# Attention in 64-query pieces, and the second gated branch added by VectorE, in an fp32 hybrid encoder step on one core

## The chip, the cores and the metric

One NeuronCore of a Trainium2 chip runs the whole program. The metric is device time in microseconds of one execution. The kernel before takes 1704.32 us (median of three runs, 1704.09 to 1705.3).

## What is computed

One step of an encoder layer for 1024 prompt tokens and 64 sample tokens (1088 in all), with D = 1024, in float32. The parts that matter here:

```python
proj = rmsnorm(x) @ w_in                      # u, v_g, q, k, v, gates
# attention: 16 query heads, 4 key heads, head dim 64, 64-query chunks,
# each sees its own chunk of keys and the two chunks (128 keys) before it
s = q @ k.T * 64**-0.5 - slope[head] * abs(distance)
m = max(max(s), sink[head]);  e = exp(s - m)
p = e / (sum(e) + exp(sink[head] - m));  o = p @ v
# sample tokens: one 64-query chunk over 128 cached keys and its own 64
merged = sigmoid(g_A) * (A @ w_pa) + sigmoid(g_B) * (B @ w_pb)   # A gated MLP, B = o
x = x + merged @ w_o
x = x + (gelu(conv3(h2 @ w_up_gate)) * (h2 @ w_up_val)) @ w_down
y = rmsnorm(x)
```

## The kernel before

**Products.** All large products have the weight as TensorE's stationary operand and the transposed activations as the moving one. Both are split into a high and a low fp32r part, and three of the four part products are made (hi hi, hi lo, lo hi). The work is cut into 56 "pairs" of 128 output channels each (`NPAIR`, L39): pairs 0 to 21 are the input projection, 22 to 25 `w_pb` ("pb"), 26 to 29 `w_pa` ("pa"), 30 to 33 `w_o` ("out"), 34 to 55 `w_up` ("up"). A pair treats its weight and activation as 2x2 blocks. A plain pair (0, 1, 22, 26 to 34) makes eight block products, the others seven by the Strassen-Winograd form, from sums of blocks that VectorE makes. The four results are called quadrants Q11, Q21, Q12, Q22; in PSUM there are three regions for them. One block product is 24 matmuls of 128x272 in four groups of six (`product`, L2123). After the pairs comes the down projection: 20 rounds of four tiles, one round per 512x256 block (L2330), and a last part in other order (L2367).

**The order** is written out by hand. Every engine walks the same grid (pair p, slot n of seven, quarter j of four), and hangs its own work on fixed places: `base`, `background` and `operands` of each engine. A tick is one quarter. TensorE puts side work between the groups of six matmuls in `background` (L2273).

**Attention** is such side work: 36 steps i, (key head b = i // 9, query tile n = i % 9), one every ten ticks (`ATT_STEP`, L134) from tick 96 on. A step takes 128 queries of the four heads of one key head. For prompt tiles 1 to 7 the keys are two tiles of 128, for n = 0 one, and for n = 8 (the sample) 128 cached and 64 own; a key outside a query's window is masked by a huge entry in the distance table, which GpSimd writes (`windows`, L1028). A head e is 2h + k; h = 0 sits on partitions 0 to 63 of the q and k tiles and h = 1 on 64 to 127.

- SyncE: `load_qk` (L777) one load of q and two of k, `load_v` (L799) one load of v per key tile, `store_o` (L812).
- TensorE: `scores` (L2193) four matmuls with 64 contraction rows, q stationary, 256 keys moving; `transpose_p` (L2208) one transpose per head and key tile, eight in a full step; `attend` (L2219) v stationary (64 columns), the transposed shares moving, for h and then for the key tile; h = 1 writes the lower 64 PSUM partitions:

```python
for h in range(2):
    for j, rows in enumerate(tiles):
        last = pe.matmul(side[64 * h:64 * h + 64, 0, 0:256].rearrange("p (k q) -> p k q", k=2),
                         v_now[0:rows, s, j, :], pt_sb[0:rows, j, 2 * h:2 * h + 2, :],
                         start=j == 0, stop=j == len(tiles) - 1)
```

- VectorE: `maxima` (L1709), `shares` (L1730). ScalarE: `exponents` (L1239), `p_out` (L1247, two 128x512 copies), `o_out` (L1255).

An f32 matmul stands in the trace as two records of its full width (x8 for four matmuls), a transpose as one.

**Operands of a stage.** When a stage begins, ScalarE makes the high parts of the seven operand blocks (`operand_hi`, L1145) and VectorE the sums (`t_sum`, L1557) and low parts (`operand_lo`, L1542, L1555). The places are tables in `operands` of each engine (L1377, L1854). For pb the low parts of blocks 5 and 4 are made within pair 22, the plain one, which doesn't use them.

**Gating.** In the pa stage VectorE multiplies each quadrant with its sigmoid gate (`gate_a`, L1790), and GpSimd adds the stored B quadrant (`merge`, L1046, add at L1052) at slots 3, 6 and, for two of the four, at the start of the next pair. The merged quadrants are the operands of the out stage: ScalarE's `operand_hi` waits for their count. The quadrant buffers are freed by it for the loads of the gates, of the B quadrants (L696 on) and of the residual (`load_residual`, L719). At the end of a pair of the out stage VectorE adds the residual to a quadrant (`residual_out`, L1666, L1674), which also frees the PSUM region for the next pair's first product.

**Down projection.** ScalarE, in order after the last pair: `convolve(21)`, `gelu(21)` (L1358, waits for both filter taps of VectorE), `down_hi_part(1)` (L1362), and so on. VectorE: the add of tile 0 to `xy` (L2015), second tap (L1830), `down_lo_part(1)` (L1844), the add of tile 1. TensorE has two PSUM sets, so tile t waits for the add of tile t - 2.

## Time and profile before

| what | value |
|---|---|
| median of the runs | 1704.32 us |
| the profiled execution | 1703.68 us, its span 1701.6 us |
| mean granted TensorE clock in it | 0.994 |
| busy share of the span | TensorE 98%, weight loads 95%, VectorE 66%, ScalarE 40%, GpSimd 5% |
| attention steps | from 118 us to 517 us |
| pb, pa, out, up stages | from 656, 745, 841 and 940 us |
| down projection | from 1412.7 us |

Times are microseconds from the start of the span. The time of the execution holds about 2 us around the span. PE is TensorE's matmuls, PEld its weight loads (which can run beside them), DVE VectorE, ACT ScalarE, POOL GpSimd, SP SyncE; a q behind a name is that engine's queue of DMA issues. "Idle before" is time in which the engine did nothing ahead of an instruction, with what released it.

### The profile page before, as it was taken

The numbers are of one execution on the slowest core, as the hardware profiler recorded it, in microseconds if no ns is written. First come the engines' busy times: TensorE is split into PE (matmuls) and PEld (weight loads), VectorE is DVE, ScalarE is ACT, GpSimd is POOL, SyncE is SP. The second block draws the span as 40 slices with busy tenths as digits, with TensorE's granted clock in tenths as the row PEclk, the third lists the DMA queues.
The fourth block names the chain that finished last, engine by engine and source line by source line (L and its number), as shares of the span: only waits on it lengthen the run. The fifth ranks groups of instructions, "written<-read, shape, count | busy, mean of one in ns | idle before, by whom it ended". The sixth has DMA issues, their size and how long they took to land.

```text
span 1701.6 us, 31439 instructions
## 1 busy us (share of the span) xinstructions
PE 1665.7 (98%) x12566; PEld 1610.8 (95%) x12566; DVE 1116.4 (66%) x2044; ACT 674.3 (40%) x1240; POOL 84.3 (5%) x143
## 2 busy tenths in 40 slices
PE   6999999999999999999999999999999999999997
PEld 6998888888889999999999999999999999999996
DVE  6666566565656878652434887777777776666665
ACT  7344454454444336442434543333333333111112
POOL 2000000000000000002212300000000000000001
PEclk8999999999999999999999999999999999999999
DMA  8443434234345855575344222222222235222122
GB/s 249 138 152 115 123 97 136 86 119 119 107 119 156 257 176 200 181 240 156 90 149 136 64 76 77 77 77 77 77 76 77 77 116 209 103 90 102 66 75 106
DMA packets 240579, 209.40 MB, mean 123 GB/s; under 512 B 24759, under 2 KB 197619, under 8 KB 240435
## 3 DMA queue, kind: packets, MB, share of 16 engines
q1 hardware_dynamic: 125806, 149.64, 26.5%
q10 hardware_dynamic: 114629, 57.76, 12.1%
q8 instruction: 100, 1.64, 0.4%
q14 instruction: 44, 0.36, 0.1%
HBM read 141.91 MB, written 65.45 MB: 122 GB/s over the span
## 4 chain that ended last, share of the span: by engine, by line
PE 75%; DVE 3%; issue 2%; ACT 1%; DMA 1%; DVEq 0%; POOL 0%; SPq 0%; ACTq 0%
PE ps L2130 55%; PE ps L2330 14%; PE ps L2225 1%; PE ps L2367 1%; PE ps L2204 1%; PE ps L2250 1%; PE ps L2216 1%; DMA r<-o_spill 1%; DVE op_lo L1555 1%; PE ps L2240 0%; PE ps L2349 0%; ACT sc_sb L1243 0%; DVE sc_sb L1721 0%; DVE y_sb L2035 0%; DVE w_lo L1516 0%
## 5 line engine op out<-in xcount | busy, mean ns | idle before, releaser
L2130 PE MATMUL ps<-op_hi,w_hi 128*128 128x272 f32 x3232 | 683.9, 293 | 11.4 <-issue 4.8
L2130 PE MATMUL ps<-op_hi,w_lo 128*128 128x272 f32 x3232 | 669.7, 289 | 0.0
L2130 PE MATMUL ps<-op_lo,w_hi 128*128 128x272 f32 x3232 | 667.8, 288 | 0.0
L2130 PEld LDWEIGHTS ps<-op_hi,w_hi 128*128 128x128 f32 x3232 | 507.4, 189 | 38.7 <-issue 36.6
L2130 PEld LDWEIGHTS ps<-op_lo,w_hi 128*128 128x128 f32 x3232 | 508.7, 189 | 0.0
L2130 PEld LDWEIGHTS ps<-op_hi,w_lo 128*128 128x128 f32 x3232 | 506.1, 189 | 0.0
L1516 DVE TENSOR_TENSOR w_lo<-raw,w_hi 128x512 fp32r<-128x512 f32 x224 | 153.5, 703 | 190.7 <-ACT w_hi L1143 190.7
L1143 ACT ACTIVATE w_hi<-raw 128x512 fp32r<-128x512 f32 x224 | 134.6, 625 | 124.5 <-PE ps L2130 90.2
L2015 DVE TENSOR_TENSOR xy<-ps,xy 128x728 f32<-128x728 f32 (+1 forms) x160 | 108.4, 719 | 79.3 <-PE ps L2330 79.3
L1220 ACT ACTIVATE u<-ps 128x544 f32<-128x544 f32 x88 | 54.8, 623 | 178.6 <-PE ps L2130 178.6
L1243 ACT ACTIVATE sc_sb<-sc_sb,att_stat 128x256 f32<-128x256 f32 (+2 forms) x144 | 69.0, 480 | 109.8 <-DVE att_stat L1727 109.8
L2330 PE MATMUL ps<-g_hi,d_hi 128*128 128x364 f32 (+1 forms) x480 | 106.7, 331 | 2.7 <-DVE xy L2015 2.6
L2330 PE MATMUL ps<-g_lo,d_hi 128*128 128x364 f32 (+1 forms) x480 | 106.3, 330 | 0.0
L2330 PE MATMUL ps<-g_hi,d_lo 128*128 128x364 f32 (+1 forms) x480 | 106.3, 330 | 0.0
L1366 ACT ACTIVATE d_hi<-d_raw 128x1024 fp32r<-128x1024 f32 x22 | 23.3, 1060 | 195.1 <-PE ps L2330 185.4
L1516 DVE TENSOR_TENSOR w_lo<-w_f,w_hi 128x512 fp32r<-128x512 f32 x132 | 87.0, 685 | 4.0 <-ACT w_hi L1143 3.4
L1143 ACT ACTIVATE w_hi<-w_f 128x512 fp32r<-128x512 f32 x132 | 78.9, 625 | 25.6 <-DVE w_f L1536 21.8
L2330 PEld LDWEIGHTS ps<-g_hi,d_hi 128*128 128x128 f32 x480 | 83.6, 189 | 3.5 <-DVE xy L2015 3.3
L2330 PEld LDWEIGHTS ps<-g_hi,d_lo 128*128 128x128 f32 x480 | 83.7, 189 | 0.0
L2330 PEld LDWEIGHTS ps<-g_lo,d_hi 128*128 128x128 f32 x480 | 83.7, 189 | 0.0
L1654 DVE TENSOR_TENSOR quad<-u,ps 128x544 f32<-128x544 f32 x69 | 49.4, 716 | 29.5 <-ACT u L1220 18.4
L1721 DVE CUSTOM_DVE_ANT_0 sc_sb<-ps,bias,sinks 128x256 f32<-128x256 f32 (+2 forms) x144 | 57.9, 459 | 0.3 <-issue 0.3
(176 smaller groups left out, 1587.5 us busy)
## 6 DMA issues: line engine op xcount, KB each, us to landing
in_spill<-quad SPq DMA_DIRECT2D x88, 272.0 KB, 2.1
raw<-in_w_up_dram ACTq DMA_DIRECT2D x44, 512.0 KB, 4.8
raw<-in_w_in_dram ACTq DMA_DIRECT2D x42, 512.0 KB, 5.7
g_spill<-value_out SPq DMA_DIRECT2D x22, 544.0 KB, 2.7
g_in<-g_spill SPq DMA_DIRECT2D x11, 1088.0 KB, 5.8
d_raw<-in_w_down_dram SPq DMA_DIRECT2D x22, 512.0 KB, 3.4
q_now<-in_spill SPq DMA_DIRECT2D x36, 128.0 KB, 2.4
gate_q<-in_spill SPq DMA_DIRECT2D x16, 272.0 KB, 8.2
```

The costliest lines, as they stand in the source:

```text
L1143: act.activation(w_hi[n][:], weight_source(p, n), copy).then_inc(s_w_hi, 1)
L1220: act.activation(two((m1c, u2, u3)[i][:]), reg[0][:, :, 0:HB], copy).then_inc(s_copied, 1)
L1243: act.activation(sc_sb[:, i % 2, e, 0:w], sc_sb[:, i % 2, e, 0:w], ACT.Exp, bias=a[:, 1, e:e + 1], accum_out=a[:, 3, e:e + 1])
L1366: act.activation(d_hi[:, blk % 2, :], d_raw[:, blk % 2, :], copy).then_inc(s_d_hi, 1)
L1516: dve.tensor_tensor(w_lo[n][:], weight_source(p, n), w_hi[n][:].bitcast(F32), ALU.subtract).then_inc(s_w, 1)
L1555: dve.tensor_tensor(op_lo[at][:, j], operand_source(g, n)[:, j], op_hi[at][:, j].bitcast(F32), ALU.subtract).then_inc(s_op, 1)
L1654: dve.tensor_tensor(two(out), two(first[:]), reg[region][:, :, 0:HB], op).then_inc(s_comb, 1)
L1721: last = dve.tensor_tensor_reduce(sc_sb[:, i % 2, e, 0:w], side[:, e // 2, 256 * (e % 2):256 * (e % 2) + w], bias[:, e, b0:b0 + w], HD ** ...
L2015: last = dve.tensor_tensor(d, v, d, ALU.add)
L2130: last = pe.matmul(out[:, h, 0:HB], (w_hi, w_lo)[a][place][:, j, :], (op_hi, op_lo)[b][at][:, j, HB * h:HB * h + HB], start=fresh and j == ...
L2204: last = pe.matmul(side[:, h, 256 * k:256 * k + w], q_now[64 * h:64 * h + 64, s, k, :], k_now[64 * h:64 * h + 64, s, 0:w], start=True, sto ...
L2330: last = pe.matmul(pset[t % 2][:, blkn, 0:t1 - t0], (d_hi, d_lo)[x][:, blk % 2, 512 * k + P * q:512 * k + P * q + P], (g_hi, g_lo)[y][g % ...
```

## The change

Four things are changed.

1. **Attention by 64 queries of two heads.** The 128 stationary columns of a score matmul are now 64 queries of both heads k = 0 and 1; a step of a full tile has two query chunks c and two h. Each chunk sees exactly its 192 keys (`SPAN`), so nothing is masked, and for n = 0 the keys that don't exist are left out (`seen`). For n = 8 there is one chunk only. The table of distances is made without GpSimd's window masks and with an added VectorE operation. The scores are 192 keys wide. Each head pair's shares are transposed in a 128-key and a 64-key part ("own"); the own parts of chunk 0 and 1 are copied to partitions 0 to 63 and 64 to 127 of a tile, and `attend` becomes four matmuls of 128 rows and four of 64 rows, all 128 columns wide, alternating in h. The copies become one of 128x512 and two of 64x256. SyncE issues two loads of q for one, and three of v for two.
2. **Merge by VectorE**, at slots (3,2), (6,1), (6,3) and (0,2) of the next pair.
3. **Low parts moved.** For pb, the low parts of blocks 5 and 4 go from pair 22 to pair 23, (0,2) and (1,2). For out and up, that of block 7a goes from (5,1) to (6,1) of the last pair ahead of the stage.
4. **ScalarE's `down_hi_part(1)`** comes before `gelu(FT - 1)`.

```diff
+def chunks_of(n):
+
+    return (0, 1) if n < NT - 1 else (0,)
+
+
+def seen(n, c):
+
+    return WINDOW - CHUNK * c if n == 0 else 0
...
-                sp.dma_start(q_now[:, s], in_spill[2 * Q_PAIR + 2 * b:2 * Q_PAIR + 2 * b + 2, :, q0:q0 + P]
-                             .rearrange("k p t -> p k t")).then_inc(s_qk_in[s], 16)
+                for c in chunks_of(n):
+                    q0 = n * P + CHUNK * c
+                    sp.dma_start(q_now[:, s, c, :].rearrange("p (k q) -> p k q", k=2),
+                                 in_spill[2 * Q_PAIR + 2 * b:2 * Q_PAIR + 2 * b + 2, :, q0:q0 + CHUNK].rearrange("k p t -> p k t"))\
+                      .then_inc(s_qk_in[s], 16)
...
-                    for m in range(len(key_rows(n))):
-                        k0 = keys_of(n)[0] + m * P
+                    for m in range(3) if n else (2,):
+                        k0 = (n - 1) * P + CHUNK * (0, 1, 2)[m]
                         sp.dma_start(v_now[:, s, m, :], vt_spill[k0:k0 + P, cols]).then_inc(s_v_in[s], 16)
...
-                if PA <= p < OUT and j == 0 and n in (3, 6):
-                    merge(4 * (p - PA) + {3: 0, 6: 1}[n])
-                if PA < p <= OUT and j == 0 and n == 0:
-                    merge(4 * (p - 1 - PA) + 2)
-                    merge(4 * (p - 1 - PA) + 3)
...
-                for j, rows in enumerate(key_rows(i % NT)):
-                    last = act.activation(pt_sb[0:rows, j, :, :], side[0:rows, j, :].rearrange("p (e q) -> p e q", e=4), copy)
+                n = i % NT
+                turned_p, own = side[:, 0, :].rearrange("p (h c q) -> p c h q", h=2, c=2), side[0:CHUNK, 1, :].rearrange("p (c q) -> p c q", c=2)
+                pt = pt_sb[:].rearrange("p (h c) q -> p c h q", h=2)
+                if 0 < n < NT - 1:
+                    act.activation(pt_sb[:].rearrange("p e q -> p (e q)"), side[:, 0, :], copy)
+                else:
+                    act.activation(pt[:, n == 0], turned_p[:, n == 0], copy)
+                for c in chunks_of(n) if n else (0,):
+                    last = act.activation(pt_own[CHUNK * c:CHUNK * c + CHUNK].rearrange("p h q -> p (h q)"), own[:, c], copy)
...
             convolve(FT - 1)
+            down_hi_part(1)
             gelu(FT - 1)
             for g in range(FT // 2):
-                down_hi_part(2 * g + 1)
+                if g:
+                    down_hi_part(2 * g + 1)
                 if g + 1 < FT // 2:
...
-                for e in range(4):
-                    head = 4 * b + 2 * (e % 2) + e // 2
-                    last = dve.tensor_tensor_reduce(
-                        sc_sb[:, i % 2, e, 0:w], side[:, e // 2, 256 * (e % 2):256 * (e % 2) + w], bias[:, e, b0:b0 + w],
-                        HD ** -0.5, sinks[:, head:head + 1], ALU.add, ALU.max, a[:, 0, e:e + 1])
+                for h in range(2):
+                    for c in chunks_of(n):
+                        e, w0 = 2 * h + c, seen(n, c)
+                        last = dve.tensor_tensor_reduce(
+                            sc_sb[:, i % 2, e, w0:SPAN], side[:, h, SPAN * c + w0:SPAN * c + SPAN], bias[:, h, w0:SPAN],
+                            HD ** -0.5, sinks[:, b, h:h + 1], ALU.add, ALU.max, a[:, 0, e:e + 1])
...
+            def merge(i):
+
+                p, q = i // 4, numbered(PA, i)[1]
+                dve.wait_ge(s_gated, i + 1)
+                dve.wait_ge(s_mb_in[i % 3], 16 * (i // 3 + 1))
+                dst = r_q[q][:, p, :]
+                dve.tensor_tensor(dst, dst, mb_buf[i % 3][:], ALU.add).then_inc(s_merged, 1)
...
-                            lows = {(1, 3): ((0, "a"),), (2, 1): ((3, "a"),), (2, 3): ((1, "a"),), (3, 3): ((0, "b"),), (5, 1): ((7, "a"),),
+                            lows = {(1, 3): ((0, "a"),), (2, 1): ((3, "a"),), (2, 3): ((1, "a"),), (3, 3): ((0, "b"),), (6, 1): ((7, "a"),),
...
-                            lows = {(1, 2): ((6, "w"),), (2, 0): ((3, "w"),), (3, 0): ((2, "w"),), (4, 2): ((5, "w"),), (5, 2): ((4, "w"),)}
+                            lows = {(1, 2): ((6, "w"),), (2, 0): ((3, "w"),), (3, 0): ((2, "w"),)}
...
-                    if (p, g) == (2, 0):
+                    if g < 3 and p == lead(g) + 1 and summed(g):
                         lows = {(0, 2): ((5, "w"),), (1, 2): ((4, "w"),)}
...
+                if stage(p) == "pa" and (n, j) in ((3, 2), (6, 1), (6, 3)):
+                    merge(4 * (p - PA) + {(3, 2): 0, (6, 1): 1, (6, 3): 2}[n, j])
+                if PA < p <= OUT and (n, j) == (0, 2):
+                    merge(4 * (p - 1 - PA) + 3)
...
-                for k in range(2):
+                for c in chunks_of(n):
                     for h in range(2):
-                        last = pe.matmul(side[:, h, 256 * k:256 * k + w], q_now[64 * h:64 * h + 64, s, k, :],
-                                         k_now[64 * h:64 * h + 64, s, 0:w], start=True, stop=True)
+                        w0 = seen(n, c)
+                        last = pe.matmul(side[:, h, SPAN * c + w0:SPAN * c + SPAN], q_now[64 * h:64 * h + 64, s, c, :],
+                                         k_now[64 * h:64 * h + 64, s, CHUNK * c + w0:CHUNK * c + SPAN], start=True, stop=True)
                 last.then_inc(s_sc, 1)
...
+                n = i % NT
+                for h in range(2):
+                    for c in chunks_of(n):
+                        e, x = 2 * h + c, sc_sb[:, i % 2, 2 * h + c]
+                        if n or c:
+                            pe.transpose(side[:, 0, e * P:e * P + P], x[:, 0:WINDOW] if n else x[:, CHUNK:SPAN], ident[:])
+                for h in range(2):
+                    for c in chunks_of(n) if n else (0,):
+                        last = pe.transpose(side[0:CHUNK, 1, (2 * c + h) * P:(2 * c + h) * P + P], sc_sb[:, i % 2, 2 * h + c, WINDOW:SPAN],
+                                            ident[:])
...
-                for h in range(2):
-                    for j, rows in enumerate(tiles):
-                        last = pe.matmul(side[64 * h:64 * h + 64, 0, 0:256].rearrange("p (k q) -> p k q", k=2),
-                                         v_now[0:rows, s, j, :], pt_sb[0:rows, j, 2 * h:2 * h + 2, :],
-                                         start=j == 0, stop=j == len(tiles) - 1)
+                for c in chunks_of(n):
+                    for h in range(2):
+                        if n or c:
+                            last = pe.matmul(side[64 * h:64 * h + 64, c, 0:P], v_now[:, s, c if n else 2, :], pt_sb[:, 2 * h + c, :],
+                                             start=True, stop=n == 0)
+                for c in chunks_of(n) if n else (0,):
+                    for h in range(2):
+                        own = slice(CHUNK * c, CHUNK * c + CHUNK)
+                        last = pe.matmul(side[64 * h:64 * h + 64, c, 0:P], v_now[own, s, 2, :], pt_own[own, h, :], start=n == 0, stop=True)
```

## Rows read from the trace of the kernel before

**Rows 1.** Busy by stretch: us, PE, PEld, DVE, ACT, POOL, PEclk, DMA share, GB/s

```profile
200.00:300.00 100.00, 99.76 (x764) 88.34 (x763) 60.78 (x205) 49.13 (x141) 0.00 (x0) 1.00 0.40 117
```

**Rows 2.** Who waited for whom on PE (total us, times, longest)

```profile
PE ps L2225 <- ACT pt_sb L1252: 2.2, 3, 0.8
```

**Rows 3.** Timeline of PE: the matmuls at four joints that waited

```profile
681.78 0.49 PE L2130 MATMUL ps<-op_hi,w_hi 128*128 128x272 f32 x2 [1.59 <-ACT quad L1309]
...
854.50 0.49 PE L2130 MATMUL ps<-op_hi,w_hi 128*128 128x272 f32 x2 [0.86 <-DVE quad L1674]
...
940.24 0.49 PE L2130 MATMUL ps<-op_hi,w_hi 128*128 128x272 f32 x2 [1.31 <-DVE quad_x L1674]
...
1424.92 1.27 PE L2330 MATMUL ps<-g_hi,d_hi 128*128 128x364 f32 x3 [2.62 <-DVE xy L2015]
```

**Rows 4.** Chain of waits, steps 34 and 35 (start us, us, what)

```profile
487.34 1.06 PE ps L2204 x8
...
491.62 0.87 PE ps L2216 x8
...
494.75 1.02 PE ps L2225 x8
...
498.23 0.85 PE ps L2204 x8
...
511.91 0.87 PE ps L2216 x8
...
515.03 2.30 PE ps L2225 x8
```

**Rows 5.** Timeline of PE around side work of steps with n = 0

```profile
213.26 0.71 PE L2204 MATMUL ps<-k_now,q_now 64*128 64x128 f32 x8
213.91 0.52 PE L2130 MATMUL ps<-op_hi,w_hi 128*128 128x272 f32 x2
...
331.08 0.65 PE L2225 MATMUL ps<-pt_sb,v_now 128*64 128x256 f32 x4
331.67 0.52 PE L2130 MATMUL ps<-op_hi,w_hi 128*128 128x272 f32 x2
```

**Rows 6.** Timeline of weight loads in the attend of step 35

```profile
515.54 0.19 PEld L2225 LDWEIGHTS ps<-pt_sb,v_now 64*64 64x64 f32 x2 [0.38 <-issue]
```

**Rows 7.** Who waited for whom on SP, 120 to 500 us

```profile
SPq L667 <- DVE quad L1654: 200.4, 49, 9.3
```

**Rows 8.** Timeline of DVE and ACT before 681.78

```profile
676.76 2.42 DVE L1555 TENSOR_TENSOR op_lo<-lo_f,op_hi 128x2176 fp32r<-128x2176 f32 x1
...
680.30 2.42 DVE L1555 TENSOR_TENSOR op_lo<-r,op_hi 128x2176 fp32r<-128x2176 f32 x1
...
681.03 0.61 ACT L1309 ACTIVATE quad<-ps 128x544 f32<-128x544 f32 x1
```

**Rows 9.** Timeline before 854.50: POOL, DVE, ACT, SP

```profile
842.71 1.74 POOL L1052 TENSOR_TENSOR r<-r,quad 128x544 f32<-128x544 f32 x1 [7.55 <-DVE r L1797]
843.14 1.88 DVE L1797 TENSOR_TENSOR r<-r,m1c 128x544 f32<-128x544 f32 x1
844.54 0.66 ACT L1175 ACTIVATE op_hi<-r 128x544 fp32r<-128x544 f32 x1 [4.01 <-POOL r L1052]
...
848.32 3.89 SPq L732 DMA_DIRECT2D quad<-xt_spill  x4
```

**Rows 10.** Timeline of DVE before 940.24

```profile
937.61 1.85 DVE L1555 TENSOR_TENSOR op_lo<-r,op_hi 128x1632 fp32r<-128x1632 f32 x1
939.38 0.71 DVE L1674 TENSOR_TENSOR quad_x<-quad_x,ps 128x544 f32<-128x544 f32 x1
```

**Rows 11.** Before 1424.92: ACT, DVE; the stretch after, columns of rows 1

```profile
1420.28 1.12 ACT L1360 ACTIVATE conv<-conv 128x1090 f32<-128x1090 f32 x1 [3.95 <-DVE conv L1830]
...
1422.37 1.22 DVE L1846 TENSOR_TENSOR d_lo<-d_raw,d_hi 128x1024 fp32r<-128x1024 f32 x1 [2.13 <-ACT d_hi L1366]
...
1424.90:1428.00 3.10, 3.08 (x10) 3.08 (x11) 3.10 (x4) 0.00 (x0) 0.00 (x0) 0.51 0.00 0
```

More of the change, by code:

```diff
@@ L17 @@
 CACHE = 128
+CHUNK, WINDOW = 64, 128
+SPAN = WINDOW + CHUNK
 HEADS, KVH, HD = 16, 4, 64
@@ L246, in qk_loads @@
 def qk_loads(i):
-    return sum(5 if m % NT == NT - 1 else 3 for m in range(i % 2, i + 1, 2))
+    return sum(5 if m % NT == NT - 1 else 4 for m in range(i % 2, i + 1, 2))
 def v_loads(i):
-    return sum(len(key_rows(m % NT)) for m in range(i % 2, i + 1, 2))
+    return sum(1 if m % NT == 0 else 2 if m % NT == NT - 1 else 3 for m in range(i % 2, i + 1, 2))
 def program(nc, x_prompt, x_sample, cache_k, cache_v, cache_conv, ln_mix_g, w_in, ln_v_g, ln_v_b, w_s, b_s,
@@ L757, in values_back @@
                 sp.dma_start(kc_in[:], cache_k[0, 0].rearrange("t h d -> t (h d)")).then_inc(s_k_in, 16)
-                sp.dma_start(sinks[:], attn_sinks.broadcast_to([P, HEADS])).then_inc(s_sinks, 16)
+                for k in range(2):
+                    sp.dma_start(sinks[CHUNK * k:CHUNK * k + CHUNK],
+                                 attn_sinks.rearrange("a (b k h) -> a k b h", b=KVH, k=2)[:, k].broadcast_to([CHUNK, KVH, 2]))\
+                      .then_inc(s_sinks, 16)
             def values_out():
@@ L1736, in shares @@
                 dve.wait_ge(s_den, 2 * i + 2)
-                for e in range(4):
-                    p = sc_sb[:, i % 2, e, 0:w]
-                    last = dve.tensor_scalar(p, p, a[:, 6, e:e + 1], None, ALU.mult)
+                for h in range(2):
+                    for c in chunks_of(i % NT):
+                        e, x = 2 * h + c, sc_sb[:, i % 2, 2 * h + c, seen(i % NT, c):SPAN]
+                        last = dve.tensor_scalar(x, x, a[:, 6, e:e + 1], None, ALU.mult)
                 last.then_inc(s_p, 1)
```

101 lines of the change are left out of this document (40 added, 61 removed).

## The prediction

> **What bounds the kernel now.** I read the busy time by stretch first: in a typical 100 us of the attention part TensorE is busy 99.76 us, VectorE 60.78 and ScalarE 49.13 [rows 1]. So a TensorE instruction saved there is time saved, and the other engines matter only where TensorE waits for them. Next, who made it wait: in the attention steps 2.2 us, for ScalarE's copies of the transposed shares [rows 2]; and four stops at stage joints, of 1.59, 0.86, 1.31 and 2.62 us [rows 3]. Then the chain of waits through two steps, which is TensorE from end to end: scores 1.06 us, transposes 0.87, attend 1.02 in a full step, and 0.85, 0.87 and 2.30 in the step of the sample tile, n = 8 [rows 4]. The reader should see that the sample tile's attend costs over twice that of a full tile, with the same eight records.
>
> **How a side group is priced.** Score groups of eight records take 1.06 us at 256 columns and 0.85 at 192 [rows 4], and 0.65 at 128 (213.26 to 213.91) [rows 5]. The difference is 0.21 us per 64 columns. Eight records at one column each per cycle of 2.4 GHz would give that sum, and so would four at half that rate, with the two h beside each other. Attend tells the two apart. In a full step, where both h are at hand, four matmuls of 256 columns take 1.02 us [rows 4]. At n = 8 the order is 128 rows, 64 rows, 128 rows, 64 rows, and they take 2.30, or 0.575 each [rows 4]; before each change of shape the weight load stands still for 0.38 us [rows 6]. So an array half handles a record in N x 0.833 ns, halves run side by side, and a run of one shape costs a fixed piece: group = r x N x 0.833 ns + c, with r records per half. Scores: c = 0.21 (4 x 0.213 + 0.21 = 1.06). Attend: c = 0.17 from 1.02 with r = 4; 0.16 from the 0.59 of n = 0 with r = 2 (331.08 to 331.67) [rows 5]; 0.15 from 0.575. I take 0.15 per run of one shape.
>
> The Trainium skill, TensorEngine Tiling (Array Packing), Key Properties, says that a change of tiling mode drains the engine, while tiles of one mode work independently. It speaks against the change: every attend gets a change of mode that full steps didn't have. By that rule, the trace agrees, with its 0.38 us stops; the price is in c already.
>
> **Attention, TensorE.** There are 28 full steps, four with n = 0, four with n = 8.
> - Scores, full: now exactly the form of the old n = 8 group, 0.85 for 1.06: -0.21 x 28 = -5.9. For n = 8 two matmuls of 192: 2 x 0.16 + 0.21 = 0.53 for 0.85, x 4 = -1.3. For n = 0 the widths 64 and 128 for two of 128: between 0 and -0.12 each; the weight load of 128 columns may bind, so -0.05 x 4 = -0.2.
> - Transposes: eight before and after in a full step, and half of the old n = 8 ones were of 64 keys too and the group took the same 0.87 [rows 4]: 0. For n = 8 four fewer at 0.87 / 8 = 0.109: -0.44 x 4 = -1.75. For n = 0 none.
> - Attend, full: four matmuls of 128 rows, r = 4 at 128 columns: 0.43 + 0.15 = 0.58. Then four of 64 rows, one in each quarter of the array if row halves run side by side as they do in the scores: r = 2, 0.21 + 0.15 = 0.36. Together 0.94 for 1.02: -0.08 x 28 = -2.2. If the row halves take turns, r = 4: 1.16, +0.14 x 28 = +3.9. No row shows quarters; I take the first, since halves run beside each other in both directions. For n = 8: 0.36 + 0.36 = 0.72 for 2.30, x 4 = -6.3. For n = 0: 0.72 for 0.59, x 4 = +0.5.
>
> Sum -17.1; with the other value -11.0.
>
> **Attention, other engines.** Scores, exponents and shares get a quarter narrower and two of four fall away at n = 8. The three copies in place of two, and a faster TensorE, can make attend wait more for ScalarE. The 2.2 us of waits [rows 2] may vanish or double; I take 0. SyncE issues two more loads per step, past the stores of quadrants; its queue stands 200.4 us in this part waiting for VectorE's quadrants [rows 7], so there is room, and the loads are issued twelve ticks, over a step, ahead. Nothing for these, nor for the distance table, which comes long before its use. Without that cover each late load would stop TensorE before its group.
>
> **The four joints.**
> - 681.78, start of pair 23. TensorE waits for ScalarE's quadrant copy (681.03 to 681.64), and ScalarE had waited for VectorE's weight sums, behind the two low parts of 2.42 us at 676.76 and 680.30 [rows 8]. The first of these stands ahead of the sum and goes to pair 23, where blocks 4 and 5 are first used in the fifth and sixth product, over 12 us in. VectorE gets free 2.4 us earlier for a stop of 1.59: -1.6. Next late would be those low parts: 4.8 us in 12.
> - 854.50, in pair 30. TensorE waits for a residual add, and that for its load, issued at 848.32 [rows 9] when the last gating freed the buffer. ScalarE stood 4.01 us for the merge on GpSimd (842.71, 1.74 us); beside it a gating on VectorE took 1.88 us [rows 9] where a like operation takes 0.71 [rows 10]. With the merge on VectorE right behind its gating, at 0.71, the high part goes out some 2 us earlier, but VectorE now has the 1.85 us of block 7a and two merges in that place. I walk VectorE's queue: the last gating comes near 847.4 in place of 847.6 to 848.3, the load 0.8 us earlier: -0.8. Sixteen merges add 16 x 0.71 = 11 us to VectorE over 100 us in which it has room; they sit behind loads of the B quadrants made a slot or more before.
> - 940.24, start of pair 34. TensorE waits for the residual add at 939.38, which stands behind block 7a's 1.85 us [rows 10]. Moved behind it: -1.3. The sums and low parts of the up stage follow in pair 34 on VectorE, so between none and all of this may come back as a later stop. I keep -1.3.
> - 1424.92. VectorE stood 2.13 us for the high part of the second block, as ScalarE made it after the gelu of 1420.28, which waits for VectorE's second tap [rows 11]. With the order turned those 2.13 go; the next adds are then some 0.4 late: -1.7 of 2.62. After the stop the granted clock was 0.51 for 3.1 us (1.2 GHz in place of 2.4) [rows 11], which lost 3.1 x 0.49 = 1.5 us. After stops of 1.59 us and less there was no such stretch at the joints, so I take -1.5 as well. Bounds for the joint: -1.1 to -4.1.
>
> Sum of the joints: -1.6 - 0.8 - 1.3 - 3.2 = -6.9.
>
> **Total.** -17.1 - 6.9 = -24.0 against 1703.68 for the profiled execution (span 1701.6): 1679.7. The median is 0.6 above it, so 1680.3; I say 1680.
>
> **Rivals.**
> 1. *Row halves take turns* in the new 64-row matmuls: +6.1, 1686. For: no row has four small blocks at once. Against: score groups of both row halves cost no more per column than a single one.
> 2. *The joints don't pay*: the stops come back behind VectorE, whose work is moved and not less, or attend waits longer for three copies. Half the joints' gain lost and the waits doubled: +3.5 + 2.2, 1686. For: at three of the joints the stop ends on VectorE's work or a wait behind it.
> 3. *Slower: no halves side by side in attend.* With h alternating from one matmul to the next, each of the eight would follow the last: r = 8 at 128 columns, 0.86 + 0.15 = 1.0 per shape and 2.0 for 1.02 in 28 steps, +27.4; n = 8: 0.58 x 2 for 2.30, -4.6; n = 0: 1.16 for 0.59, +2.3. In all +25.1 for the -8.0 above: 1713. It decides in attend, from about 0.85 us over today's 1.02 on. For: the old n = 8 group ran one by one. Against: there the shape changed each time; the old full group had the h one after the other in program order and still ran them side by side. The Trainium skill's page TensorE: Matmul & The Clock Gate, Part 3, has it that matmuls start and end in strict program order. [...]
> 4. *It doesn't do what it says*, for example TensorE's saving is given back as waits for loads or for VectorE: within 0.2% of before, 1702 to 1707.
>
> **Chances.** Forecast 0.63, its own range 1675 to 1684 (waits -2.2 to +2.2, joints -1 to +2). Rival 1 0.13, rival 2 0.13, both together (1692) 0.03, rival 3 0.04, other slower ways 0.02, rival 4 0.02. A range of 1674 to 1691 leaves about 2 in 10 out with my own doubt of the prices. About 0.2% is what a measurement of this kernel can tell from no change: faster 0.92, same 0.02, slower 0.06.
>
> **What would show it.** Right: full attend near 0.94 us (x16), full scores 0.85, sample attend near 0.7; no stop over 0.5 us at the first three joints, one under 1.3 in the down projection and no stretch there at half clock. Attend at 1.16 is rival 1, at 2.0 rival 3. Wrong: stops of TensorE ahead of scores or attend that add up to over 5 us, or pairs 34 to 36 with new stops.

## The result and the profile after

The changed kernel took 1687.97 us, beside 1704.34 for the kernel before: ratio 0.9893, 95% interval 0.9871 to 0.9915. That median counts one slow execution of 4100.05 us, which no experiment here explains and which the ratio leaves out; the four others took 1681.86 to 1688.63, median 1687.31. Run again (after_again) it took 1687.08, from 1683.04 to 1690.88, beside 1703.74: 0.9898 (0.9879 to 0.9918). So it is faster by 1.0 to 1.1%, 16 to 17 us. The time lies inside the predicted 1674 to 1691, but 7 to 8 us above the predicted 1680, and outside the 1675 to 1684 that the forecast gave as its own range. Two things need explaining: why the joints paid less than forecast, and why runs of one kernel now differ by 7 to 8 us where those of the kernel before differ by 1 to 4.

Everything below on the changed kernel is from after_again's profiled execution: 1683.04 us, span 1681.2. It is the fastest of its four runs, so it shows the change without the part that comes and goes.

An attention stretch by windows (columns as in [rows 1]):

```profile
200.00:300.00 100.00, 99.97 (x851) 91.88 (x850) 59.56 (x208) 49.09 (x150) 0.00 (x0) 1.00 0.42 119
```

and who waited for whom in the attention part, TensorE's row and SyncE's (total us, times, longest):

```profile
PE ps L2243 <- ACT pt_own L1239: 2.0, 3, 0.7
...
SPq L663 <- DVE quad L1646: 173.2, 48, 7.7
```

TensorE is as full as in [rows 1] and does more records (851 for 764), its waits for ScalarE's copies are 2.0 us for the 2.2 of [rows 2], and SyncE still stands 173.2 us in that part [rows 7]. So in this execution neither the third copy nor the added loads cost anything in the attention part.

One full attend, timeline of TensorE and of its weight loads (start us, us, then engine, line, operation, tiles; in brackets the idle time before and what ended it):

```profile
144.84 0.66 PE L2243 MATMUL ps<-pt_sb,v_now 128*64 128x128 f32 x8
145.43 0.45 PE L2248 MATMUL ps<-pt_own,v_now 64*64 64x128 f32 x8
145.81 0.39 PE L2137 MATMUL ps<-op_hi,w_hi 128*128 128x272 f32 x1
...
145.43 0.21 PEld L2248 LDWEIGHTS ps<-pt_own,v_now 64*64 64x64 f32 x8 [0.17 <-issue]
```

From start to start the 128-row run takes 0.59 us and the 64-row run 0.38, together 0.97 for the 1.02 of [rows 4]. Eight records of 128 columns in 0.38 us is the price for r = 2 (0.36 was forecast; 0.58 if the row halves took turns): the four quarters run beside each other. In the chain of waits of the run with the attention alone a score group of 192 columns takes 0.85:

```profile
430.01 0.85 PE ps L2212 x8
```

The largest single term of the forecast is the attend of the sample tile, n = 8. Here it is in after_again, in step 35 (timeline of TensorE):

```profile
500.69 0.44 PE L2243 MATMUL ps<-pt_sb,v_now 128*64 128x128 f32 x4
501.06 0.44 PE L2248 MATMUL ps<-pt_own,v_now 64*64 64x128 f32 x4
501.43 0.52 PE L2137 MATMUL ps<-op_hi,w_hi 128*128 128x272 f32 x2
```

That is 0.74 us (500.69 to 501.43) for the 2.30 of [rows 4]; 0.72 was forecast.

At the four joints of [rows 3] TensorE now stops like this (timeline of TensorE, its matmuls that waited; pairs 30 and 34 begin without a stop):

```profile
665.31 0.36 PE L2137 MATMUL ps<-op_hi,w_hi 128*128 128x272 f32 x1 [0.96 <-ACT quad L1299]
...
948.83 0.49 PE L2137 MATMUL ps<-op_hi,w_hi 128*128 128x272 f32 x2 [1.59 <-ACT gate_out L1299]
953.53 2.05 PE L2290 MATMUL ps<-ident,stat 128*128 128x128 f32 x16 [0.71 <-POOL stat L1061]
...
1404.58 0.43 PE L2351 MATMUL ps<-g_hi,d_hi 128*128 128x364 f32 x1 [0.41 <-DVE xy L2022]
...
1417.86 0.43 PE L2351 MATMUL ps<-g_hi,d_hi 128*128 128x364 f32 x1 [0.84 <-DVE xy L2022]
```

The stop of pair 23 is 0.96 for 1.59, those of pairs 30 and 34 are gone, a new one of 1.59 us stands at the start of pair 35 with a wait of 0.71 us for GpSimd behind it, and the down projection stops for 0.41 and 0.84 instead of 2.62, with no stretch at half clock: from 1404 to 1424 the granted clock is 1.00 throughout, where [rows 11] had 0.51.

**A ledger by stage.** The length of a row runs from the start of its first pair to the start of the pair behind its last one; a pair starts with its first product matmul in the trace. In us, for the one profiled execution of each kernel:

| stage | before | after_again | joints_only | attention_only | wait_raw | combined |
|---|---|---|---|---|---|---|
| pairs 3 to 21 | 547.76 | 530.72 | 547.93 | 530.71 | 530.65 | 530.66 |
| pair 22 | 25.80 | 25.17 | 25.72 | 25.11 | 24.89 | 24.06 |
| 23 to 25 | 63.45 | 63.23 | 63.20 | 67.89 | 64.15 | 63.14 |
| 26 to 29 | 96.22 | 96.21 | 96.22 | 96.22 | 96.28 | 96.21 |
| 30 to 33 | 98.79 | 96.22 | 96.21 | 97.93 | 96.22 | 96.21 |
| 34 to 36 | 72.43 | 73.58 | 73.58 | 72.43 | 73.58 | 73.59 |
| from pair 55 to the end of the span | 310.09 | 307.81 | 307.28 | 310.34 | 307.5 | 307.56 |

Pairs 37 to 54 take 378.84 in all six. Pairs 0 to 2 take 84.1 to 85.9 and vary from run to run. The stop at the start of pair 23 falls into the row "pair 22", and so on.

### The profile page after: what moved, and what is told of

Its sections match the earlier page's. It is cut to its first block, busy times and chain, and to the rows that moved or that the text cites. A ratio compares the mean times of both kernels' runs of the same rounds, so it can differ in the third digit from the quotient of the medians.

```text
span 4098.3 us, 31903 instructions
## 1 busy us (share of the span) xinstructions
PE 4081.1 (100%) x12774; PEld 3818.7 (93%) x12774; DVE 1127.7 (28%) x2037; ACT 674.4 (16%) x1256; POOL 54.3 (1%) x125
## 4 chain that ended last, share of the span: by engine, by line
PE 100%; issue 0%; DMA 0%; DVE 0%; ACT 0%; POOLq 0%; POOL 0%; ACTq 0%; DVEq 0%
PE ps L2137 75%; PE ps L2351 15%; PE ps L2388 2%; PE ps L2213 2%; PE ps L2271 1%; PE ps L2232 1%; PE ps L2229 1%; PE ps L2243 1%; PE ps L2248 1%; PE ps L2261 1%; PE ps L2370 1%; PE ps L2075 1%; PE ps L2187 0%; PE ps L2290 0%; PE ps L2173 0%; PE ps L2279 0%
## 5 line engine op out<-in xcount | busy, mean ns | idle before, releaser
L2137 PE MATMUL ps<-op_hi,w_hi 128*128 128x272 f32 x3232 | 1393.6, 550 | 5.6 <-issue 5.6
L2137 PE MATMUL ps<-op_hi,w_lo 128*128 128x272 f32 x3232 | 1384.7, 547 | 0.0
L2137 PE MATMUL ps<-op_lo,w_hi 128*128 128x272 f32 x3232 | 1384.3, 547 | 0.0
L2137 PEld LDWEIGHTS ps<-op_hi,w_hi 128*128 128x128 f32 x3232 | 1093.9, 368 | 50.0 <-issue 42.8
L2137 PEld LDWEIGHTS ps<-op_lo,w_hi 128*128 128x128 f32 x3232 | 1117.0, 376 | 0.0
L2137 PEld LDWEIGHTS ps<-op_hi,w_lo 128*128 128x128 f32 x3232 | 1109.6, 373 | 0.0
L2351 PE MATMUL ps<-g_hi,d_lo 128*128 128x364 f32 (+1 forms) x480 | 239.7, 654 | 0.0
L2351 PE MATMUL ps<-g_lo,d_hi 128*128 128x364 f32 (+1 forms) x480 | 239.4, 653 | 0.0
L2351 PE MATMUL ps<-g_hi,d_hi 128*128 128x364 f32 (+1 forms) x480 | 239.4, 653 | 0.0
L2351 PEld LDWEIGHTS ps<-g_hi,d_lo 128*128 128x128 f32 x480 | 166.9, 351 | 36.2 <-issue 30.7
```

The costliest lines, as they stand in the source:

```text
L2137: last = pe.matmul(out[:, h, 0:HB], (w_hi, w_lo)[a][place][:, j, :], (op_hi, op_lo)[b][at][:, j, HB * h:HB * h + HB], start=fresh and j == ...
L2351: last = pe.matmul(pset[t % 2][:, blkn, 0:t1 - t0], (d_hi, d_lo)[x][:, blk % 2, 512 * k + P * q:512 * k + P * q + P], (g_hi, g_lo)[y][g % ...
```

## The experiments

### The change again, and each half alone

after_again is the changed kernel. attention_only is the changed kernel with the four joints put back; joints_only is the kernel before with the four joints changed. The edits at the joints, shortened:

```diff
-pool.tensor_tensor(dst, dst, mb_buf[i % 3][:], ALU.add)           # merge
+dve.tensor_tensor(dst, dst, mb_buf[i % 3][:], ALU.add)            # at (3, 2), (6, 1), (6, 3), (0, 2)
-(5, 1): ((7, "a"),)                                               # VectorE's low parts
+(6, 1): ((7, "a"),)
-pair 22: (4, 2): ((5, "w"),), (5, 2): ((4, "w"),)
+pair 23: (0, 2): ((5, "w"),), (1, 2): ((4, "w"),)
+down_hi_part(1)
 gelu(FT - 1)
-down_hi_part(1)
```

> The changed kernel, unaltered, for a profile in which TensorE runs at full clock (the one taken with the result didn't). My theory: attention saves about 17 us and the joints about 7 of 1704.3; near 1680 to 1688 us in all. Full attend near 0.94 us if the four small blocks run in four quarters of the array, near 1.16 if the row halves take turns (rival 1). The joints at pairs 23, 30 and 34 without a stop over 0.5 us. The median of 1688 in place of 1680 leaves some 8 us: either the attend group is at 1.16 (+6), or a joint kept its stop, or a stretch at 1.2 GHz has come in somewhere; the stops of TensorE and the granted clock by stretch tell.

> The kernel before with the attention in 64-query pieces alone; merge, low parts and down_hi_part as before. My theory: -17 us, 1687, or -11, 1693, if the row halves take turns. If the attention change gives nothing and all comes from the joints (rival 4): 1704.

> The kernel before with the old attention, and the merge by VectorE, the moved low parts and the earlier down_hi_part. My theory: -7 us, 1697. If the stops come back behind VectorE (rival 2): 1701 to 1704.

Measured, beside 1703.74 for before: attention_only 1689.22 (0.9906, 0.989 to 0.9922), joints_only 1699.89 (0.9975, 0.9966 to 0.9985), after_again 1687.08. In the ledger the attention gives 17.0 us in its own stage, as forecast (-17.1), with the joints or without. The joints alone give 3.9 of the 6.9. Beside the new attention, after_again less attention_only in the ledger without pairs 23 to 25, they give 3.0.

attention_only has a loss that no other column shows: 67.89 us for pairs 23 to 25, 4.4 more than before. Its profiled execution took 1689.8. The timelines of ScalarE and of TensorE there, in pair 25:

```profile
722.71 1.15 ACT L1135 ACTIVATE w_hi<-raw 128x512 fp32r<-128x512 f32 x2 [6.35 <-DMA raw<-in_w_pa_dram]
...
727.79 0.56 PE L2136 MATMUL ps<-op_hi,w_hi 128*128 128x272 f32 x1 [3.07 <-DVE quad L1657]
```

the stretch behind the stop (columns as in [rows 1]):

```profile
728.10:730.70 2.60, 2.60 (x13) 2.60 (x13) 2.60 (x2) 2.60 (x3) 0.00 (x0) 0.50 0.50 192
```

and the loads issued from 709 to 711 us (KB each, median us from issue to landing):

```profile
lo_f<-a_spill SPq DMA_DIRECT2D x1, 1088.0 KB, 7.9
...
raw<-in_w_pa_dram ACTq DMA_DIRECT2D x2, 512.0 KB, 9.0
```

The same issues in after_again, from 710 to 712 us:

```profile
lo_f<-a_spill SPq DMA_DIRECT2D x1, 1088.0 KB, 8.7
...
raw<-in_w_pa_dram ACTq DMA_DIRECT2D x2, 512.0 KB, 6.2
```

ScalarE issues the two halves of the weights for pair 26, and SyncE issues lo_f, the first operand of the third stage, 1 us behind the first half and its two r loads behind that. Which lands first changed: the weights' median is 9.0 us here and 6.2 there (their second half took 12.98 and 7.9 us from issue), and lo_f came in 7.9 and not 8.7. ScalarE, in order, stood 6.35 us, TensorE 3.07, and the stretch behind the stop ran at a granted clock of 0.50 (1.2 GHz), which lost another 2.6 x 0.5 = 1.3 us: 4.4 together, the whole loss of that row. That makes a suspect for the spread of 8 us.

### Does the late load make the spread?

wait_raw holds SyncE's loads back until the weights are in:

```diff
 if p == FIRST_PAIR[g] - 1 and (n, j) == (1, 0):
+    if g == 2:
+        sp.wait_ge(s_raw, 32 * (PA + 1))
     load_first_operand(g, src)
```

> The changed kernel with one wait more: SyncE issues its loads of the first operands of the third stage (lo_f, r) only when pair 26's weights have landed. Theory: the forecast of 1680 missed most because in some executions the second half of those weights (12.98 us from issue to landing, for some 8 in others) lands behind SyncE's loads, ScalarE stands 6.35 us and TensorE about 3.2, with 1.2 us lost at half clock behind it. Then with the wait every run is within 1 us of 1682, the median is 1682 to 1683.5 and pairs 23 to 26 take 63.2 us as in the good run. Rival: the spread of 1683 to 1691 comes from something else; then the runs spread as before and the median is 1687 +- 2. A third way: the held loads themselves come late for the residual adds or the gating of pair 26; then a new stop of TensorE in pairs 26 to 30 and a median above 1684.

Measured: 1683.31, runs from 1682.94 to 1684.41, ratio 0.9878 (0.9861 to 0.9894). The spread of 8 us is 1.5; in the seven other kernels below that hold loads back and ran four times it is 0.7 to 4.0, widest in pool_first (3.97), which lets lo_f go, and in no_down (3.33), which doesn't. The median is 3.8 below that of the changed kernel, though the two intervals overlap. The median is as expected, but not every run was within 1 us of 1682, and pairs 23 to 25 took 64.15, not 63.2. The third way is near the cause: a held load comes late, here lo_f for ScalarE, and the stop stands in pair 25 (timelines of ScalarE and TensorE of wait_raw):

```profile
722.27 2.02 ACT L1156 ACTIVATE op_hi<-lo_f 128x2176 fp32r<-128x2176 f32 x1 [3.88 <-DMA lo_f<-a_spill]
...
725.76 0.36 PE L2139 MATMUL ps<-op_hi,w_hi 128*128 128x272 f32 x1 [0.67 <-DVE quad L1648]
```

What is shown: the late landing in one execution of 1689.8 us, and that the spread is smaller in all eight kernels that hold loads back. That the longer executions of the changed kernel had the late landing is inferred, since none of them was profiled. Why the kernel before doesn't have it (its weights took 6.1 us there with the same order of issues) was not tested. Both stay open.

### Why pair 23 still stops

ScalarE's timeline of after_again before the stop at 665.31, and VectorE's:

```profile
656.52 2.02 ACT L1154 ACTIVATE op_hi<-lo_f 128x2176 fp32r<-128x2176 f32 x1 [3.52 <-DVE lo_f L1586]
...
660.06 2.00 ACT L1154 ACTIVATE op_hi<-r 128x2176 fp32r<-128x2176 f32 x1
661.97 0.61 ACT L1122 ACTIVATE w_hi<-raw 128x512 fp32r<-128x512 f32 x1
664.03 0.63 ACT L1122 ACTIVATE w_hi<-w_f 128x512 fp32r<-128x512 f32 x1 [1.44 <-DVE w_f L1528]
664.56 0.60 ACT L1299 ACTIVATE quad<-ps 128x544 f32<-128x544 f32 x1
```

```profile
662.62 0.69 DVE L1508 TENSOR_TENSOR w_lo<-raw,w_hi 128x512 fp32r<-128x512 f32 x1 [2.02 <-ACT w_hi L1122]
```

VectorE did get free, and then stood 2.02 us for ScalarE, whose high parts of the same two blocks (2.0 us each) had not moved. And the stop went from 1.59 to 0.96 by the attention, not by this move: it is 1.50 us with the joints alone, and with the attention alone (timeline of TensorE of attention_only)

```profile
664.35 0.36 PE L2136 MATMUL ps<-op_hi,w_hi 128*128 128x272 f32 x1 [0.90 <-ACT quad L1312]
```

wait_raw_hi moves ScalarE's two high parts too:

```diff
-  (2, 0): ((2, "w"),), (4, 0): ((5, "w"),), (5, 0): ((4, "w"),)     # ScalarE, pair 22
+  (2, 0): ((2, "w"),)
+  pair 23: (0, 1): ((5, "w"),), (1, 0): ((4, "w"),)
```

and no_lows54 takes VectorE's half of the move back, on wait_raw.

> As wait_raw, and ScalarE's high parts of weight blocks 5 and 4 for the third stage follow VectorE's low parts into pair 23. Theory: the stop at the start of pair 23 (1.1 us with the new attention) stayed when VectorE's low parts were moved, because ScalarE works in order and those two high parts of 2.0 us each stood ahead of its gate multiplies and of the copy that TensorE waits for. Moved as well, the stop falls below 0.3 us and the time by 0.9 to 1.2 us against wait_raw. Rival: the stop is set by VectorE's sums or by the loads of the quadrants; then it stays at 1.1 +- 0.2 and the time is that of wait_raw within 0.4. A cost may come: ScalarE has 4 us more in pair 23 ahead of the products of blocks 5 and 4; if these are late, TensorE stops over 0.5 us in pair 23.

> wait_raw with VectorE's low parts of blocks 5 and 4 back in pair 22 (all the other joints as changed). Theory: this move does next to nothing, since ScalarE's high parts set the stop at pair 23: 1.06 us (as with the attention alone) for 0.84, so pairs 22 to 23 take 25.1 us for 24.89 and the median is 1683.5 +- 0.4. By the prediction it would be +1.6. Its second use: of the four joints' edits only this one was in every run in which GpSimd's power on 128x8 took 11.46 us. If that hangs on the order of VectorE's work at pair 34 it is 11.46 here too; if it is 6.72 here, the cause lies in something that this edit shifts.

Measured: no stop at pair 23 in wait_raw_hi, pair 22 24.06 us for 24.89; the median 1682.98, which is 0.3 less and not 0.9 to 1.2. In no_lows54 pair 22 takes 25.17, +0.28; its median is 1684.56 (1684.24 to 1684.93), above the expected 1683.5 +- 0.4, with 0.8 us more in pairs 23 to 25 too, which the edit doesn't explain. So in pair 22 VectorE's move alone is worth 0.3 us beside wait_raw and nothing clear in the ledger above (25.80 to 25.72 with the old attention, 25.11 to 25.17 with the new), and with ScalarE's 1.1, where the prediction had 1.6 for VectorE's alone.

### The order of attend's matmuls

```diff
-for c in chunks_of(n):
-    for h in range(2):
+for h in range(2):
+    for c in chunks_of(n):
```

> As wait_raw, with the two heads in the outer loop and the chunks of keys in the inner one in both runs of the new attend, so that four (or two) neighbours in program order have the same column half. Theory: matmuls of different array parts overlap whatever their order, so the full attend stays near 0.59 for the 128-row run and 0.38 for the 64-row run, 0.97 us together, and pairs 3 to 22 take the same time within 1 us. Rival (strict program order, only neighbours overlap): the turned order puts like column halves next to each other, the 128-row run goes from 0.59 to about 0.8 or more and attend to over 1.2 us, which over 20 pairs is 5 us or more.

Timeline of TensorE in h_first, the step shown above:

```profile
144.99 0.67 PE L2245 MATMUL ps<-pt_sb,v_now 128*64 128x128 f32 x8
145.59 0.45 PE L2250 MATMUL ps<-pt_own,v_now 64*64 64x128 f32 x8
145.97 0.40 PE L2139 MATMUL ps<-op_hi,w_hi 128*128 128x272 f32 x1
```

0.60 and 0.38 us, for 0.59 and 0.38; pairs 3 to 21 took 531.18 for 530.65, in the one execution of h_first. In the 128-row run two matmuls of one column half now stand next to each other, and the halves still overlap. In the 64-row run each quarter has one matmul in either order, so there the order was hardly put to the test. Rival 3 of the prediction fails in both orders. The Trainium skill, TensorE: Matmul & The Clock Gate, Part 3, says that matmuls start and end in strict program order, and in the same place that those of different tiles overlap. By that rule, both traces agree: a strict order of starts and ends leaves room for the overlap seen here, so it doesn't speak for rival 3.

### What the stop in pair 35 is

The rows of after_again ahead of the stop at 948.83, ScalarE:

```profile
947.54 0.63 ACT L1122 ACTIVATE w_hi<-w_f 128x512 fp32r<-128x512 f32 x1 [3.72 <-DVE w_f L1528]
948.08 0.60 ACT L1299 ACTIVATE gate_out<-ps 128x544 f32<-128x544 f32 x1
```

TensorE waits for the copy of 948.08, which stands behind a weight that waits for VectorE's sum (946.75, behind two low parts of 2.41 us). combined puts that sum one low part earlier, keeps ScalarE's move of wait_raw_hi (not shown again), and lets lo_f go at once:

```diff
-places = ((2, 2), (3, 0), (5, 0), (6, 2)) if plain(p) else ...
+places = ((2, 2), (3, 0), (4, 1) if p == UP else (5, 0), (6, 2)) if plain(p) else ...
 load_first_operand(g, src)
+if g == 2: sp.wait_ge(s_raw, 32 * (PA + 1))     # only ahead of the r loads
```

> The changed kernel with three edits: SyncE waits for pair 26's weights ahead of its r loads only, no longer ahead of lo_f; ScalarE's high parts of blocks 5 and 4 follow into pair 23; and the third weight sum for pair 35 stands one low part earlier on VectorE (before the 2.41 us of block 5's low part, not behind it). Theory: (1) lo_f comes early again, the stop of 0.8 us at 725 goes and pairs 23 to 26 take 63.2 to 63.4 us where wait_raw took 64.15; (2) no stop over 0.3 us at pair 23; (3) ScalarE gets its weight sum 2.4 us earlier, the gate copy that TensorE waited for is no longer behind it, and the stop at 948 falls from 1.7 to below 0.6 us. Sum against wait_raw_hi (1682.98): -0.8 for (1), -1.2 for (3): 1681.0, range 1680.2 to 1682. Rival to (3): the stop is VectorE's total of some 19 us between the last residual add and pair 35, not the order; then the stop moves to the next product and is 1.2 us or more, and 34 to 37 stays 73.6 us. Rival to (1): lo_f beside the weights delays them again; then runs of 1685 or more appear.

Measured: 1681.41, from 1680.76 to 1683.64, ratio 0.9868 (0.9852 to 0.9883): the lowest median here, clearly below the kernel before; its interval still overlaps that of the changed kernel a little. (1) and (2) came true: 63.14 us and no stop at pair 23. (3) did not: the stop fell to 0.25 and 0.27 us, but pairs 34 to 36 took 73.59, as in every kernel above with this joint changed. So the median lies in the expected range without the 1.2 us of (3). The rival gave that length, by VectorE's total; in the trace the wait went to GpSimd. TensorE's timeline of combined, then GpSimd's:

```profile
945.53 0.52 PE L2138 MATMUL ps<-op_hi,w_hi 128*128 128x272 f32 x2 [0.25 <-DVE w_lo L1509]
...
949.07 0.40 PE L2138 MATMUL ps<-op_hi,w_hi 128*128 128x272 f32 x1 [0.27 <-DVE w_lo L1509]
...
951.58 0.60 PE L2291 MATMUL ps<-ident,stat 128*128 128x128 f32 x3 [1.49 <-POOL stat L1063]
```

```profile
939.08 11.46 POOL L1062 TENSOR_TENSOR stat<-stat,columns 128x8 f32<-128x8 f32 x1 [11.38 <-DVE stat L1806]
950.51 1.02 POOL L1063 TENSOR_TENSOR stat<-stat,columns 64x1 f32<-64x1 f32 x1
```

The second norm's row factors go from VectorE to GpSimd, which raises 128x8 numbers to a power in 11.46 us, and TensorE's spreading of the factors waits for them. In the changed kernel's chain of waits this is a piece of the path, from the row means to TensorE:

```profile
940.73 0.16 DVE stat L1804
...
941.03 11.46 POOL stat L1060
952.49 1.00 POOL stat L1061
...
953.53 2.05 PE ps L2290 x16
```

In the kernel before the same two operations took 9.16 us together for 12.48, and TensorE didn't wait for them (GpSimd's timeline of before):

```profile
959.67 6.72 POOL L1074 TENSOR_TENSOR stat<-stat,columns 128x8 f32<-128x8 f32 x1 [12.19 <-DVE stat L1802]
966.35 2.44 POOL L1075 TENSOR_TENSOR stat<-stat,columns 64x1 f32<-64x1 f32 x1
```

From the start of pair 34 the factors are ready after 28.6 us before (968.79 less 940.24) and after 32.5 in after_again (953.49 less 920.97). This also explains why wait_raw, whose trace has half clock (1.2 GHz) for 3.2 us in pair 34 and almost no stop in pair 35, took the same 73.58: what TensorE loses ahead of that point is hidden behind GpSimd. The kernel before had such a stretch in pair 34 too, 13 us behind the stop at 940.24, and the prediction missed it. The two stretches, wait_raw's and then before's:

```profile
934.60:937.80 3.20, 3.20 (x17) 3.20 (x16) 3.20 (x5) 1.41 (x3) 0.00 (x0) 0.50 0.00 0
...
953.60:956.70 3.10, 3.10 (x15) 3.10 (x15) 3.10 (x3) 1.25 (x2) 0.00 (x0) 0.50 0.00 0
```

### Is it GpSimd's own time?

pool_first is combined with one more wait, which makes VectorE stand still while GpSimd works:

```diff
 if (p, n, j) == (UP, 3, 1):
     mean_in()
+    dve.wait_ge(s_r1, 1)
```

> The combined kernel with one wait more: behind the two small operations that hand the row means to GpSimd, VectorE waits until GpSimd has made the row factors. In every kernel with the moved low parts GpSimd's power on 128x8 took 11.46 us and the next 1.02 (6.72 and 2.44 in the kernel before), TensorE waited for it 0.7 to 1.5 us, and pairs 34 to 37 took 73.58 us whatever was done to VectorE's order. Theory: the power is short in itself and is held off by VectorE's unbroken row of operations with two inputs in SBUF (back to back, from 0.15 us ahead of it to 11 us behind). Then with VectorE standing still it takes under 2.5 us, the wait of TensorE for GpSimd goes, VectorE loses 1.5 to 3 us of which part comes back as stops at pair 35's first products, and pairs 34 to 37 take 71.3 to 73.0 us: median 1679.1 to 1680.8 for 1681.4. Rival: the 11.46 us are GpSimd's own (its program); then VectorE stands 12.5 us, TensorE stops some 8 us or more in pair 35, and the time rises to about 1690.

GpSimd's timeline of pool_first, then VectorE's and TensorE's:

```profile
938.61 1.66 POOL L1062 TENSOR_TENSOR stat<-stat,columns 128x8 f32<-128x8 f32 x1 [11.38 <-DVE stat L1806]
940.24 0.53 POOL L1063 TENSOR_TENSOR stat<-stat,columns 64x1 f32<-64x1 f32 x1
```

```profile
940.80 2.42 DVE L1548 TENSOR_TENSOR op_lo<-lo_f,op_hi 128x2176 fp32r<-128x2176 f32 x1 [2.27 <-POOL stat L1063]
...
947.43 0.52 PE L2139 MATMUL ps<-op_hi,w_hi 128*128 128x272 f32 x2 [2.61 <-DVE w_lo L1509]
```

1.66 and 0.53 us for 11.46 and 1.02: the operation is short, and VectorE's unbroken row of work held it off for nearly 10 us. The Trainium skill, SBUF — State Buffer, Who interferes with whom, says that a VectorE instruction with two inputs in SBUF contends with a GpSimd instruction that reads SBUF, and that the one that issues second is blocked until the first has finished. By that rule, the traces agree on who blocks whom; but VectorE's operations there are 0.7 to 2.4 us each, and the 11.46 us span ten of them, which the rule by itself doesn't give.

The time did not follow: 1683.14 (1681.88 to 1685.85), and pairs 34 to 36 took 74.19, outside the 71.3 to 73.0 expected. The wait for GpSimd was gone, and the 2.27 us that VectorE stood came back as a stop of 2.61 us for its weights. So at this place there are two chains of nearly one length: VectorE's parts for pair 35 and GpSimd's factors. Relieving VectorE's alone (combined) gained nothing. pool_first relieves GpSimd's at VectorE's cost, so what a short power would give by itself was not measured.

### Three joints taken back, on wait_raw

no_merge has the second branch added by GpSimd as before, no_lows7 block 7a's low part at (5, 1), no_down `gelu(21)` ahead of `down_hi_part(1)`: the lines of the first diff, each turned round alone. These three, no_lows54, combined and pool_first ran on another chip than wait_raw, wait_raw_hi and h_first.

> wait_raw (1683.3) with the second branch added by GpSimd, as in the kernel before. Theory: the stop of 0.86 us in pair 30 comes back with about that size, pairs 30 to 34 take 97.1 to 97.3 us for 96.22, and the median is 1684.2. Rival: the stop went with the changed pair lengths, as in the run with attention alone, not with the merge; then no stop at pair 30 and a median of 1683.3 +- 0.4. A cost is possible the other way: VectorE is 11 us less busy in pairs 26 to 30, which no stage waits for: 0.

> wait_raw with block 7a's low part ahead of the residual add again. Theory: the stop of 1.2 to 1.4 us at the start of pair 34 comes back, and what took its place (the stop of up to 1.75 us in pair 35, or the stretch at half clock behind the mean squares with 1.5 us lost) goes again: pairs 30 to 34 +1.4 to +1.7, pairs 34 to 37 -1.15 (72.4 us for 73.58), median 1683.3 + 0.3 to 0.6. By the prediction's sum it would be +1.3 (1684.6). Rival: the stop in pair 35 has nothing to do with the move and both stay: +1.3 as well, but with 34 to 37 still at 73.6 us.

> wait_raw with the down projection's high part behind the last gelu again. Theory: VectorE's wait for the second block's high part returns, stops in the down projection go from 1.3 us together (0.55 + 0.1 + 0.7) to 3.9 us (2.78 + 1.27, as with the attention alone): median 1683.3 + 2.5 = 1685.8, without a stretch at half clock; with one (as in the kernel before) another 1.2 to 1.5 on top. Rival: the down stage's gain came from the earlier stages' new timing; then the median is within 0.5 of 1683.3.

| kernel | median (runs) | its stage, wait_raw in brackets | predicted cost | shown |
|---|---|---|---|---|
| no_merge | 1683.73 (1682.88 to 1685.16) | pairs 30 to 33 96.28 (96.22) | +0.8 | +0.1 |
| no_lows7 | 1684.69 (1683.64 to 1684.99) | 30 to 33 97.68 (96.22), 34 to 36 72.97 (73.58) | +1.3 | +0.85 |
| no_down | 1686.3 (1684.53 to 1687.86) | from 55 on 309.8 (307.5) | +3.2 | +2.3 |

TensorE's stops that came back, no_lows7 first, then no_down:

```profile
923.26 0.49 PE L2139 MATMUL ps<-op_hi,w_hi 128*128 128x272 f32 x2 [1.31 <-DVE quad_x L1668]
...
950.49 0.49 PE L2139 MATMUL ps<-op_hi,w_hi 128*128 128x272 f32 x2 [0.87 <-ACT gate_out L1301]
```

```profile
1406.30 0.60 PE L2351 MATMUL ps<-g_hi,d_hi 128*128 128x364 f32 x2 [2.61 <-DVE xy L2022]
...
1419.36 0.43 PE L2351 MATMUL ps<-g_hi,d_hi 128*128 128x364 f32 x1 [0.60 <-DVE xy L2022]
```

The column "shown" is the change in these rows of the ledger, one execution each. By the medians the three differ from wait_raw by 0.4, 1.4 and 3.0 us, and all three intervals overlap wait_raw's.

The merge on GpSimd brings no stop back: with the new timing the stop of 0.86 us in pair 30 is gone whichever engine adds. Block 7a's move is real at its own joint (1.46 us), and 0.61 of it is given back in pairs 34 to 36, where the expectation had 1.15: with the move undone the stop in pair 35 is still 0.87. The down projection's turned order is worth 2.3 us. No profiled execution with the new attention had a half-clock stretch there, in either order, and the stretch had cost the kernel before nothing of its own: attention_only, with the old order, ran at full clock there and took as long (310.34 for 310.09), with a second stop of 1.11 us behind the one of 2.62 instead (timeline of TensorE):

```profile
1424.64 0.43 PE L2350 MATMUL ps<-g_hi,d_hi 128*128 128x364 f32 x1 [1.11 <-DVE xy L2021]
```

## Why the prediction was right, and where it was off

- **Attention, -17.1.** Shown: -17.04 in the ledger, -17.05 without the joints. The price model held: 0.85 for a full score group, 0.59 + 0.38 for attend where 0.58 + 0.36 was forecast, 0.74 for the sample tile's where 0.72 was. Part of the agreement is luck. Added up over pairs 3 to 21, the scores gave 7.3 us (7.4 forecast), the transposes 1.7 (1.75) and attend 7.2 (8.0), together 16.2; another 0.9 came off the products and waits between the groups, which the sum didn't have. Rival 1 (row halves take turns, 1.16 us) and rival 3 (2.0 us) are refuted by 0.97, rival 3 also with the order turned.
- **Other engines, 0.** Held within the attention. Missed outside it: in some executions of the kernels with the new attention pair 26's weights land late, 4.4 us in the one that shows it. The sum had no term for a load whose landing can go either way. The run that holds SyncE back makes it the likely reason why the median is 1687 and not 1683; its part in each single run is inferred.
- **Pair 23, -1.6.** The step that failed is "VectorE gets free 2.4 us earlier", taken as the end of the stop. VectorE did get free, but the stop ended on ScalarE, which is in order and still made the high parts there. Shown: 0 to -0.3 for the move, -1.1 with ScalarE's share moved too. The sign "no stop over 0.5 us at the first three joints" failed here, with 0.96.
- **Pair 30, -0.8.** The stop went, but not by this edit: +0.1 when the merge alone is taken back, and the attention alone has no stop there either. My walk through VectorE's queue priced one cause of a stop that several changes remove.
- **Pair 34, -1.3.** -1.46 at the joint and +0.61 behind it, net -0.85; I wrote that between none and all might come back as a later stop. The prediction looked for it on VectorE. The last word had GpSimd, whose power operation went from 6.72 to 11.46 us beside a VectorE without a pause: a term that was not in the sum. The sign of being wrong "pairs 34 to 36 with new stops" came true, with 1.59 and 0.71.
- **Down projection, -3.2.** -2.28 in the ledger and 2.3 by taking it back. The forecast was 1.7 of stops and 1.5 of clock. Shown is that all of it is stops: 2.61 + 0.60 in no_down for 0.39 + 0.52 in wait_raw, and 2.62 + 1.11 in attention_only for 0.41 + 0.84 in after_again. At half clock TensorE came later to the next tile and did not stop for it; at full clock it stopped 1.11 us. So the clock's 1.5 us, carried over whole, was a gain that the next wait takes back. The prediction's "after stops of 1.59 us and less there was no such stretch" left out the 3.1 us at 0.50 in pair 34 of the kernel before; in wait_raw what such a stretch loses there is hidden behind GpSimd's factors.
- **Sum.** The ledger gives -17.0 - 0.6 - 0.2 - 2.6 + 1.15 - 2.3 = -21.6, and +1.2 of variation in and ahead of the first pairs makes the -20.4 of the spans. Forecast was -24.0. That compares the fastest of four executions with one of the kernel before; by the medians the gain is 16 to 17 us. Of rival 2 the half about the joints came true: 3.9 us of 6.9 when changed alone, 3.0 beside the new attention. Its doubled waits of attend did not. So the 1686 that it named is close to the measured 1687 by another sum: 3 to 4 us less at the joints and, as far as inferred, some 4 from the late load.

## What to carry to other kernels

Before moving one engine's work past a joint, walk every in-order queue that feeds the stopped copy: the partner engine's half of the same blocks kept the stop here. Loads of two queues issued some 1 us apart landed in either order here (9.0 and 7.9 us, or 6.2 and 8.7), so let the load that something waits for first go ahead alone; with a wait of one line the spread of four runs was 1.5 us for 8. And when several edits of one stage all end at the same length to 0.01 us, look for a chain that none of them touches.

## What was not expected of the hardware

- A GpSimd operation on 128x8 numbers took 1.66 us with VectorE standing still, 6.72 in the kernel before and with the attention alone, and 11.46 in the ten others, with VectorE's rows around it nearly alike. What decides between 6.72 and 11.46 was not found: undoing any one joint left 11.46. One thing goes with it: ScalarE's 2.0 us high part starts 2.5 us into the operation in the two with 6.72, and 0.2 to 1.8 us into it in the ten. No run tests whether that matters.
- Four 64x64 quarters of the array work beside each other: eight f32 records of 128 columns in 0.38 us, their fixed part included.
- The same two loads of 512 KB took 6.2 or 9.0 us (median) with the same neighbours issued in the same order.
